# Value products head by head with both parts of the values as one stationary operand, and weight chunks handed over by halves

## The reference

```python
h = rmsnorm(x, g_pre_mix)
q_sb, k_sb, v_sb, q_mla, ckv, k_rope, gate_a, gate_b = split(h @ w_in)
# branch A, 8 heads x 64: stick-breaking, strictly causal
a = where(visible, exp(log_sigmoid(z) + suffix), 0);  o_sb = a @ v_sb
# branch B, 8 heads: latent attention, softmax, causal by chunks of 64
o_lat = softmax(q_lat @ ckv.T + q_rope @ k_rope.T) @ ckv;  o_mla = o_lat @ w_uv
mix = (sigmoid(gate_a) * (o_sb @ w_proj_sb) + sigmoid(gate_b) * (o_mla @ w_proj_mla)) @ w_out
x = x + rmsnorm(mix, g_post_mix)
u = rmsnorm(x, g_pre_ffn) @ w_up;  uc = causal_conv3(u)
x = x + rmsnorm((gelu(gate) * val) @ w_down, g_post_ffn)
x = x + sigmoid(x @ w_ple_gate) * (p[i] @ w_ple_proj)
```

## Time and profile before

| what | value |
|---|---|
| median of 3 runs (lowest to highest) | 1856.55 us (1854.4 to 1856.71) |
| the profiled execution, and its span | 1855.66 us, 1853.8 us |
| busy in the span: DVE, ACT, POOL | 927.1, 559.6, 1070.4 us |
| mean granted clock of PE | 0.999 |
| value matmuls: 192 of 512 columns, 96 of 256 | mean 408 and 280 ns each |
| attention phases with their projections | about 40 to 300 us and 960 to 1230 us |

### The profile page before, as it was taken

How to read it: one execution, slowest core, us unless ns; L and a number is a source line. 1 busy time by engine, 2 the same in 40 slices (tenths; PEclk the granted TensorE clock), 3 DMA queues, 4 the chain that set the end, 5 groups by cost and what they waited for, 6 DMA issues and landing times.

```text
span 1853.8 us, 33791 instructions
## 1 busy us (share of the span) xinstructions
PE 1830.7 (99%) x14262; PEld 1775.2 (96%) x14262; DVE 927.1 (50%) x1634; ACT 559.6 (30%) x1197; POOL 1070.4 (58%) x994
## 2 busy tenths in 40 slices
PE   9999999999999999999999999999999999999999
PEld 8998989999999999999999999899999999999999
DVE  5666775232755532523556767752336555235143
ACT  4444543112422221202344344531133222122021
POOL 7685634656555555556666854346456555555564
PEclk9999999999999999999999999999999999999999
DMA  5242212333222222223342421212422222222222
GB/s 181 95 127 73 70 41 71 101 107 125 69 92 91 82 91 92 85 80 99 97 146 89 126 75 58 69 58 92 151 81 69 92 92 82 90 92 87 80 87 94
DMA packets 76231, 170.49 MB, mean 92 GB/s; under 512 B 6384, under 2 KB 34160, under 8 KB 76080
## 3 DMA queue, kind: packets, MB, share of 16 engines
q1 hardware_dynamic: 68752, 160.79, 26.7%
q10 hardware_dynamic: 7328, 7.54, 1.2%
HBM read 156.41 MB, written 9.79 MB: 90 GB/s over the span
## 4 chain that ended last, share of the span: by engine, by line
PE 89%; DVE 5%; POOL 2%; ACT 2%; DMA 1%; issue 1%; SPq 0%; DVEq 0%; ACTq 0%; POOLq 0%
PE ps L1550 75%; PE ps L1585 2%; PE ps L1713 2%; POOL wsp L611 2%; PE ps L1671 2%; DVE xn L1083 1%; DVE xT L1422 1%; DVE mix L1419 1%; PE ps L1762 1%; PE ps L1768 1%; PE ps L1624 1%; DVE R L1083 1%; POOL wsp L605 1%; DVE xT L1240 1%; PE ps L1736 1%
## 5 line engine op out<-in xcount | busy, mean ns | idle before, releaser
L1550 PE MATMUL ps<-xn,wsp 128*128 128x272 f32 x7824 | 1003.7, 289 | 7.4 <-POOL wsp L611 2.6
L1550 PEld LDWEIGHTS ps<-xn,wsp 128*128 128x128 f32 x7824 | 986.9, 189 | 11.6 <-issue 5.5
L611 POOL TENSOR_TENSOR wsp<-raw,wsp 128x256 fp32r<-128x256 f32 (+1 forms) x578 | 726.3, 1278 | 22.3
L605 POOL CAST wsp<-raw 128x512 fp32r<-128x512 f32 (+2 forms) x372 | 319.5, 873 | 660.0 <-DMA raw<-in_wstream 565.4
L1550 PE MATMUL ps<-R,wsp 128*128 128x272 f32 x3840 | 486.2, 288 | 0.1
L1550 PEld LDWEIGHTS ps<-R,wsp 128*128 128x128 f32 x3840 | 482.7, 188 | 1.2 <-DVE xT L1112 0.5
L1083 DVE SCALAR_TENSOR_TENSOR R<-ps,R 64x256 fp32r<-64x256 f32 (+11 forms) x264 | 129.8, 510 | 77.6 <-ACT R L679 26.0
L1438 DVE TENSOR_TENSOR mix<-ps,rstd 128x272 f32<-128x272 f32 x88 | 38.8, 441 | 202.6 <-PE ps L1550 192.3
L968 ACT ACTIVATE mix<-vv 128x2 f32<-128x2 f32 x88 | 18.0, 204 | 363.0 <-DVE mix L1440 363.0
L1083 DVE SCALAR_TENSOR_TENSOR R<-mix,R 128x544 fp32r<-128x544 f32 (+2 forms) x86 | 74.7, 869 | 82.0 <-ACT R L989 66.9
L1446 DVE SCALAR_TENSOR_TENSOR ps<-mix,vv,ps 128x546 f32<-128x546 f32 x88 | 69.4, 788 | 55.6 <-ACT ps L977 55.6
(11 more groups left out here) (230 smaller groups left out, 1473.9 us busy)
## 6 DMA issues: line engine op xcount, KB each, us to landing
raw<-in_wstream SPq DMA_DIRECT2D x233, 512.0 KB, 3.5
raw<-in_wstream SPq DMA_DIRECT2D x48, 128.0 KB, 2.6
raw<-in_wstream SPq DMA_DIRECT2D x16, 384.0 KB, 3.0
raw<-in_kc SPq DMA_DIRECT2D x8, 512.0 KB, 3.7
raw<-in_vc SPq DMA_DIRECT2D x8, 512.0 KB, 4.5
xT<-in_x_in SPq DMA_DIRECT2D x8, 272.0 KB, 6.6
out_k_out<-mix ACTq DMA_DIRECT2D x8, 272.0 KB, 3.2
xT<-in_x_in SPq DMA_DIRECT2D x1, 2176.0 KB, 9.4
```

The costliest lines, as they stand in the source:

```text
L605: ins = nc.gpsimd.tensor_copy(dst[:, 0, f], part[:, f])
L611: ins = nc.gpsimd.tensor_tensor(dst[:, 1, f], part[:, f], dst[:, 0, f].bitcast(F32), ALU.subtract)
L1550: mm = pe.matmul(z[:, h], w[:, x, (k0 + k) * P:(k0 + k + 1) * P], rhs[:, y, k, h * HT:(h + 1) * HT], start=(k == 0 and (x, y) == (0, 0)), ...
```

## The change

It edits the order of the value products, the layout of their operands and their read-out, and the handover of weight chunks.

- `pv` becomes one tile per head, "pv0" and "pv1", both at `start+5`. The stationary operand holds the high and the low part of one head's 64 value columns side by side (128 columns). Per key block `kb` two matmuls run over it, with the high and with the low part of the weights, of (4 - kb) x 128 columns: 512, 384, 256 and 128. High-part results land in partitions 0 to 63, low-part results in 64 to 127, and low x low is now computed too.
- `at` is laid out by key blocks, so that each matmul reads one contiguous run; head 1 is stored and computed with its query blocks in reverse order, and its transposes are placed in reverse.
- The read-out of a head is one copy of 64x512 by ACT, and on DVE a subtraction of 64x512, a wait for it, and an addition of partitions 64 to 127.
- Chunks in `HALVED` (c, kr, q, k, v, qr, qn, ga and gb 0 to 3, proj 0 and 1, pleg) are cast and subtracted half by half; POOL raises `w_half` after the first half and `w_lo` after the second, and `project` and `together` wait for them at k = 0 and k = 4. The special case of the first two chunks goes.

```diff
+FINE = [c for n, c in enumerate(STREAM) if n <= ST_AT[("proj", 1)] or n >= ST_AT[("down", len(FFN_PARTS) - 1, 4)]]
+HALVED = [c for c in FINE if c[0] not in ("ukuv", "K", "V", "CT", "CR", "CC", "pp", "down")]
...
-        at = reg(b1, 2, 2, ATW)
+        at = reg(b1, 2, 2 * ATW)
...
-            o = qb * (qb + 1) // 2 * P
-            return at[:, x, :, o:o + P * (qb + 1)]
+            a = at[:, x, qb * P:(qb + 1) * P]
+            return bass.AP(tensor=a.tensor, offset=a.offset,
+                           ap=[a.ap[0], [(2 * ATW // P - 1 - 5 * qb) * P, 2], [3 * P, qb + 1], [1, P]])
+
+        def at_keys(x, r, kb):
+
+            o = (2 * ATW // P - 4 - 3 * kb if r else 4 * kb) * P
+            return at[:, x, o:o + (QB - kb) * P]
+
+        def turned(ap, r):
+
+            z = ap.rearrange("p (b q) -> p b q", q=P)
+            return z[:, ::-1] if r else z
+
+        def v_parts(buf, i, y):
+
+            return buf[:, i, :, y]
...
-        AHEAD = {start(br, t) + d: [("pv" + h + br, t)] for br in "sm" for t in range(PAIRS) for h, d in (("a", 3), ("b", 5))}
+        AHEAD = {start(br, t) + 5: [("pv0" + br, t), ("pv1" + br, t)] for br in "sm" for t in range(PAIRS)}
...
+                        if ch in HALVED:
+                            for i in range(2):
+                                if layer == 0 and c == 0 and i == 1:
+                                    pool.wait_ge(raw_in[0], 16)
+                                f = slice(i * w // 2, (i + 1) * w // 2)
+                                nc.gpsimd.tensor_copy(dst[:, 0, f], part[:, f]).then_inc(S["w_hi"], 1)
+                                highs += 1
+                                pool.wait_ge(S["w_hi"], highs)
+                                for j in range(2):
+                                    f = slice((2 * i + j) * w // 4, (2 * i + j + 1) * w // 4)
+                                    ins = nc.gpsimd.tensor_tensor(dst[:, 1, f], part[:, f], dst[:, 0, f].bitcast(F32), ALU.subtract)
+                                ins.then_inc(S["w_lo" if i else "w_half"], 1)
+                            continue
...
                     def pv_tile(t):
+                        if t[0] == "pv0s" and t[1] == 2:
+                            act.wait_ge(pre["qr_in"], QR_MOVES * (layer + 1))
+                        r = int(t[0][2])
                         act.wait_ge(S["p_done"], AT[t] + 1)
-                        if t[0] == "pvas" and t[1] == 2:
-                            act.wait_ge(pre["qr_in"], QR_MOVES * (layer + 1))
-                        o, q = (o_sb if t[0][3] == "s" else o_ml), slice(0, SEQ // 2) if t[0][2] == "a" else slice(SEQ // 2, SEQ)
-                        for r in range(2):
-                            ins = ac(o[64 * r:64 * r + 64, 0, t[1], q], bank(t)[64 * r:64 * r + 64, 256 * r:256 * r + 256], ACT.Copy)
-                        ins.then_inc(S["act_read"], 1)
+                        z = turned(bank(t)[0:64], r)
+                        o = (o_sb if t[0][3] == "s" else o_ml)[64 * r:64 * r + 64, 0, t[1], 0:SEQ]
+                        ac(turned(o, 0), z, ACT.Copy).then_inc(S["act_read"], 1)
...
-                        elif t > 0 and qb in (0, 2):
-                            act.wait_ge(S["p_done"], AT[(("pva" if qb == 0 else "pvb") + br, t - 1)] + 1)
+                        elif t > 0 and qb == 0:
+                            act.wait_ge(S["p_done"], AT[("pv1" + br, t - 1)] + 1)
...
                     def pv_tile(t):
                         dve.wait_ge(S["act_read"], aread(t))
-                        o, q = (o_sb if t[0][3] == "s" else o_ml), slice(0, SEQ // 2) if t[0][2] == "a" else slice(SEQ // 2, SEQ)
-                        for r in range(2):
-                            lo(o[64 * r:64 * r + 64, 1, t[1], q], bank(t)[64 * r:64 * r + 64, 256 * r:256 * r + 256],
-                               o[64 * r:64 * r + 64, 0, t[1], q], "dve_read" if r else None)
+                        r, z = int(t[0][2]), bank(t)
+                        o = (o_sb if t[0][3] == "s" else o_ml)[64 * r:64 * r + 64, :, t[1], 0:SEQ]
+                        lo(turned(o[:, 1], 0), turned(z[0:64], r), turned(o[:, 0], 0), "pv_low")
+                        dve.wait_ge(S["pv_low"], PV_AT[t] + 1)
+                        v.tensor_tensor(turned(o[:, 1], 0), turned(z[64:128], r), turned(o[:, 1], 0).bitcast(F32),
+                                        ALU.add).then_inc(S["dve_read"], 1)
...
-                            lo(at_view(1, qb), z_view(n, P * (qb + 1)), at_view(0, qb), "at_lo")
+                            v.tensor_tensor(at_view(1, qb), z_blocks(n, qb), at_view(0, qb).bitcast(F32), ALU.subtract).then_inc(S["at_lo"], 1)
...
+                    def split(chunk, k, first):
+
+                        if chunk in HALVED:
+                            if k == 0:
+                                pe.wait_ge(S["w_half"], HALVED.index(chunk) + 1)
+                            elif k == KT // 2:
+                                pe.wait_ge(S["w_lo"], ST_AT[chunk] + 1)
+                        elif first:
+                            pe.wait_ge(S["w_lo"], ST_AT[chunk] + 1)
+
...
                             for kb in range(qb + 1):
-                                mm = pe.transpose(ps[:, ZB + 2 * (n % 2) + r, kb * P:(kb + 1) * P], x[:, r, kb * P:(kb + 1) * P], ident)
+                                j = qb - kb if r else kb
+                                mm = pe.transpose(ps[:, ZB + 2 * (n % 2) + r, j * P:(j + 1) * P], x[:, r, kb * P:(kb + 1) * P], ident)
...
                     def pv(t):
 
-                        br, p = t[0][3], t[1]
-                        n = start(br, p) + (1 if t[0][2] == "a" else 3)
-                        val, o = (v_s if br == "s" else vm)[:, p % 2], 0 if t[0][2] == "a" else 3 * P
+                        br, p, r = t[0][3], t[1], int(t[0][2])
+                        val = (v_s if br == "s" else vm)[:, p % 2]
                         banks_free(t)
-                        if t[0][2] == "a":
+                        if r == 0:
                             pe.wait_ge(S["dve_read"], dread(("vt" if br == "s" else "kv", p)))
-                        pe.wait_ge(S["at_lo"], n + 1)
-                        z, blocks = bank(t).rearrange("p (r q) -> p r q", r=2), 2 if t[0][2] == "a" else QB
-                        for kb in range(blocks):
-                            for i, (x, y) in enumerate(PARTS):
-                                if kb == blocks - 1:
-                                    mm = pe.matmul(z[:, :, P:2 * P], val[:, x, kb], at[:, y, :, o + 2 * kb * P:o + (2 * kb + 1) * P],
-                                                   start=False, stop=(i == 2))
-                                else:
-                                    a = at[:, y, :, o:o + 2 * (blocks - 1) * P].rearrange("p r (b q) -> p r b q", b=2)
-                                    mm = pe.matmul(z.rearrange("p r (b q) -> p r b q", b=2), val[:, x, kb],
-                                                   a[:, :, :, kb * P:(kb + 1) * P], start=(kb == 0 and i == 0), stop=False)
+                            pe.wait_ge(S["at_lo"], start(br, p) + QB)
+                        for kb in range(QB):
+                            w = (QB - kb) * P
+                            z = bank(t)[:, 0:w] if r else bank(t)[:, 512 - w:512]
+                            for x in range(2):
+                                mm = pe.matmul(z, val[:, 2 * kb + r].rearrange("p x f -> p (x f)"), at_keys(x, r, kb),
+                                               start=(kb == 0 and x == 0), stop=(kb == QB - 1 and x == 1))
                         mm.then_inc(S["p_done"], 1)
```

More of the change, by code:

```diff
@@ L177, in build @@
         b2 = b1 + 4 * ATW
-        v_s = reg(b2, 2, 2, QB, P)
+        v_s = reg(b2, 2, 2 * QB, 2, 64)
         kn = reg(b2, 2, 2, SEQ)
@@ L239, in z_view, with z_blocks @@
             return ps[:, ZB + 2 * (n % 2):ZB + 2 * (n % 2) + 2, 0:w]
+        def z_blocks(n, qb):
+            return z_view(n, P * (qb + 1)).rearrange("p r (b q) -> p r b q", q=P)
         def bt_view(n, w):
@@ L310, in ahead @@
             return AHEAD.get(s, [])
+        PV_AT = {t: n for n, t in enumerate([t for s in range(STEPS) for t in ahead(s) if t[0][0:2] == "pv"])}
         def after(s):
@@ L568, in _ @@
                         part = raw[:, n_raw % SLOTS, 1, 0:w]
-                        if layer == 0 and ch in STREAM[0:2]:
-                            if c == 0:
-                                pool.wait_ge(pre["c_in"], 16)
-                            else:
[L573 to L582, removed]
+                        if layer == 0 and c == 0:
+                            pool.wait_ge(pre["c_in"], 16)
+                        else:
+                            pool.wait_ge(raw_in[n_raw % SLOTS], 16 * LOADS[n_raw])
+                        if layer == 0 and c == 1:
+                            pool.wait_ge(S["xn_lo"], KT - 1)
                         if ch == ("CR", 0):
@@ L600, in _ @@
```

(19 more changed lines are left out.)

30 lines of the change are left out of this document (15 added, 15 removed).

## The result

The changed kernel takes 1861.45 us (median of 8 runs, 1859.06 to 1862.19), the one before 1856.72 us in the same rounds (8 runs, 1853.09 to 1857.55). The ratio is 1.0024, 95% interval 1.0015 to 1.0034: slower by 4.5 us, a quarter of a per cent. The interval leaves out 1, so the loss is clear, but small. The forecast was 1859.2 us. The profiled execution took 1862.00 us, 1860.1 of them the span; before, the span was 1853.8, so 6.3 us are to be explained.

The account below looks back on a forecast made before the run. PE was taken to bound the kernel (busy 1830.7 of 1853.8 us). Terms -18.2 + 1.9 + 1.6 + 19.9 - 2.6 - 1.5 + 1.5 = +2.6 us gave 1859.2 us against the median 1856.55; overall range 1844 to 1867, the forecast's own 1854 to 1865.

Parts of the forecast that it names:

- 12 early groups: Value matmuls at `start+3` that PE waits for nothing behind; their gain of 1.14 us each was taken whole.
- part 2: Two attention-loop iterations where PE, 1.14 us earlier without early value matmuls, runs into DVE: 1.6 us come back.
- step 5: Iteration of the loop over `units`: `("q",2)` opens on the pair's banks; wait hidden behind filler, 0.4 us to spare.
- step 14: Iteration of the loop over `units`: `("ot",0)` takes pv0s,2's bank and waits for its read; 1.8 us for two layers.
- Part 1: Value products on PE: 18.2 us of early groups go, 1.9 us come at `start+5`; a pair takes 2.62 us.
- Part 3: Reading out a head: ACT copy 0.60 us, DVE subtraction 0.68 and addition 0.67; ends 0.42 and 0.84 per DVE read.
- slower rival: Evacuation of a head: DVE's reads cost 0.84 us instead of 0.68, 8.0 us more, 1867 us; chance 0.15.
- Part 4: PSUM banks: other neighbours make PE wait for both readers of a bank's last tile; new waits sum to 19.9 us.
- step 9: Iteration `start("s",1)+5`: `("v",3)` waits for pv1s,1's bank behind late DVE, 5.5 and 5.9 us, 11.4 counted in all.
- first rival: The wait behind pair 1's value products does not come; 11.4 and 1.5 us of clock fall away, 1846.3 us; chance 0.20.
- Part 6: PE's clock: 1.5 us go with a covered weight wait; 1.5 us charged behind one new long wait, ends 0 and 3.0.
- Part 5: Weight chunks by halves: first half ready 2.3 us earlier, three PE waits for weights vanish, 2.6 us go.

Follow-up runs that it names:

- after once more: The changed kernel, unaltered, measured again beside the kernel before to see how well its loss repeats: 1862.08 us, ratio 1.0023.

## Why the prediction was right, and where it wasn't

The forecast, 1859.2 us, is 2.3 us below the median of the result, and the places that it named are those where PE gained and lost. Change of each place, from the starts of the steps' scores in the two timelines, both layers summed, in us (rounded, so the columns miss their sums by 0.1):

| place | predicted | measured |
|---|---|---|
| start, up to the scores of step 0 | -0.6 | -1.1 |
| 12 early groups | -13.7 | -13.1 |
| steps 3 and 12 (part 2) | -2.9 | -3.6 |
| step 5 | +0.2 | +1.7 |
| steps 9 and 10, clock included | +9.7 | +11.7 |
| step 14 | +2.0 | +2.7 |
| step 18 | +3.3 | +3.4 |
| step 23 | +0.2 | +0.2 |
| steps 27 and 31 | +2.9 | +2.9 |
| step 35 and all behind it | +1.4 | +1.4 |
| sum | +2.6 | +6.3 |

- *The total is closer than its terms.* +2.6 was the small difference of 22 us of gains and 25 of losses, and single places are off by up to 2.0 us. That the sum came out on the right side of zero is in part luck; that it would be near zero is not.
- *Part 1, the matmuls*: a pair takes 2.58 us, predicted 2.62. The unknown form, 384 columns, goes at 0.18 us (two of them take 0.36 and 0.35 us from start to start), halfway between its neighbours as taken. The early group was worth 1.09 where 1.14 was put. The "some 7 us" by the formula of the Trainium skill (TensorE: Matmul & The Clock Gate, "Back-to-back issue gap") are worked out wrongly: they price only the kernel after by the formula. With both kernels priced by it a pair falls from 3.25 to 2.17 us, an estimate of 17.2 us saved, 0.9 more than the 16.3 of the sum.
- *The start* gained 0.5 us more than its wait for weights: the first filler begins at 7.32 us instead of 7.77 and then waits less for DVE. Its begin lies between 7.1 and 7.8 in all the profiled executions, so nothing is read into that.
- *Part 3, the read-outs*: 0.678 and 0.694 us on DVE, 0.591 on ACT; predicted 0.68, 0.67 and 0.60. Half the partitions don't make an operation shorter: 64x512 takes 0.678 us, 128x512 took 0.679. This decided against the slower rival (0.84).
- *Part 4, the banks*: step 9 waits 5.41 and 5.53 us, predicted 5.5 and 5.9; step 18 1.36, less than the 1.53 put. The rotation in front of DVE's read-outs and the bank behind them are each shown as causes (1.40 us are left without the one, 3.1 to 3.4 without the other, nothing without both). The first rival, 1846.3 us, is about what the kernel takes when that wait is taken away (1847.45).
- *Part 6, the clock, is the term that was mis-sized.* I charged one layer 1.5 us, because of two waits for weights one had been followed by the low level. Both layers paid, 2.5 and 1.6 us. Together that is 4.1 us, so the end of the range, 3.0, was also too low. The short waits of before were a poor guide to waits four times as long. The sentence on the Trainium skill (TensorE: Matmul & The Clock Gate, Part 1) had both layers pay, and here the trace agrees. The 1.5 us per layer that I worked out for it from the earlier trace rows were too small: 3.0 against 4.1 us.
- *Step 5 is a miss of 1.5 us.* I called the wait hidden with 0.4 us to spare even where DVE starts 0.4 us late. DVE was later: it reached its first read-out only at 84.46, 3.57 us after the first value matmul. In the timeline of DVE at step 5, the rotation of `qr` 0 and the scans behind it:
```profile
79.20 1.02 DVE L1183 TENSOR_TENSOR mix<-mix 128x544 f32<-128x544 f32 x1
80.25 1.14 DVE L1184 TENSOR_TENSOR mix<-mix 128x544 f32<-128x544 f32 x1
...
82.36 2.17 DVE L1271 TENSOR_TENSOR_SCAN xT<-xT 128x256 f32<-128x256 f32 x2
84.46 0.66 DVE L1112 SCALAR_TENSOR_TENSOR R<-ps,R 64x512 fp32r<-64x512 f32 x1
...
86.59 0.69 DVE L1209 TENSOR_TENSOR R<-ps,R 64x512 fp32r<-64x512 f32 x1
```
Before, the same two additions took 0.81 and 0.72 us, and the scans:
```profile
83.79 1.64 DVE L1240 TENSOR_TENSOR_SCAN xT<-xT 128x256 f32<-128x256 f32 x2 [0.33 <-ACT xT L825]
```
In both kernels the rotation begins 2.5 us before the first value matmul, so DVE had as much time as before and needed more: the scans end 2.6 us after that matmul before, 3.6 us after it now. In the timeline of POOL its casts and subtractions run on through this rotation, where before POOL stood idle from 81.4 to 83.1. That this made DVE's operations longer was read from the trace and not tried by an experiment.
- *Step 14* stands for 1.01 us in layer 0 where 0.86 was put, and costs 2.7 us in all where 2.0 was put. ACT's copy is named as the releaser, but it had ended 0.6 us before. DVE's addition for the first head ended at 168.60, and PE goes on 0.1 us later: it is the bank of pv0s,2 again. With the rotation later DVE's scans in front of that took 1.27 us instead of 1.64, and the wait was 0.72. Why they differ is not shown.
- *Part 5, the halves*: in the kernel before they bring 4 to 4.6 us, here nothing, since the larger wait covers what they take away. Both were in the working (2.6 and 1.5 us, the last two waits vanishing "anyway").

The expected gain of the change is there, 16.7 us less of columns and waits behind them. It was turned into standing still: PE waits for a bank whose last reader is the last of four operations in a row on DVE. The same products are now read in two heads with an addition more each, and at step 9 that row starts behind the rotation, 4.0 us later than without it.

## What to carry to other kernels

When work is moved off the bounding engine onto one that has time to spare, look for who takes the bank or buffer next, and in which order the relieving engine gets to it: its share of busy time says nothing, the place in its queue does. A long wait on TensorE can have a second price in the clock behind it (1.6 to 2.7 us behind waits of about 5 us here), so first try to move other work of the slow engine behind the hand-over, or to give the next tile another bank; where neither can be, even useless transposes in the gap paid here. Change one place of a dealt-out order at a time, since each edit deals all later banks anew.

## What the runs showed of the hardware

- **The clock and idle time.** PE's waits of 5.41, 5.53 and 4.03 us were followed by the 1.2 GHz level, as was one of 3.40 (granted 0.76 over the next 7 us, so part of it). The 48 filler matmuls behind, 6.26 us at full clock, took 8.79, 7.85, 8.63 and 7.77 us; in after once more, behind waits of 5.63 and 4.99 us, 7.96 and 9.00. Waits of 3.13 and 3.25 us weren't followed by it, and with 3.5 us of transposes in the gap neither layer's clock fell. Yet before, a wait of 1.19 us was also followed by it: the length of the last wait alone doesn't tell.
- **DVE and POOL on the same memory.** In the timeline of POOL around step 9, first while DVE rotates, then while it reads from PSUM:
```profile
115.96 4.22 POOL L640 TENSOR_TENSOR wsp<-raw,wsp 128x256 fp32r<-128x256 f32 x4
...
121.50 2.77 POOL L640 TENSOR_TENSOR wsp<-raw,wsp 128x256 fp32r<-128x256 f32 x4
```
Four subtractions take 4.22 us beside DVE's additions of two operands in SBUF (1.07 to 1.15 us each; at step 5 of before, mostly with POOL idle, 0.72 to 0.81), and 2.77 beside read-outs with one operand in PSUM, which stay at 0.68. The Trainium skill (GPSIMD Engine Reference, "1. Specifications") says that the two engines contend where DVE has two inputs in SBUF; the trace agrees, and both take about one and a half times as long. No run tries it by itself.
- **Pace of matmuls by columns**, with a weight load each: 0.108 us for 128, 0.120 for 256, 0.18 for 384, 0.230 for 512. In these rows going from 128 to 256 columns costs 0.01 us.
